# The second block's first projections on unscaled tiles, with their additive part from small products; two norms in one factor; the convolution begun on ScalarE

## The chip, the cores and the metric

The kernel runs on one core of a Trainium2 chip as one program. The metric is the device time of one execution in microseconds. Three runs of the kernel before took 2013.33, 2015.04 and 2018.52 us; the median is 2015.04.

## The reference

Two models follow each other on a sequence of 512 tokens of width 1024. The first has two layers, each with a root-mean-square norm, an input projection, three mixers, an output projection, a second norm and a gated feed-forward part of width 2816. After them stands a final norm. The second model is one block. What bears on the change is its start:

```python
x = rmsnorm(x, final_norm)                          # end of the first model
mod = silu(c) @ w_c + b_c                           # second model
shift, scl, gate = split(mod, 3)
h = rms_norm(x, g_pre) * (1 + scl) + shift
xa, za, q, k, v, zb, ga, gb = split(h @ w_in)
xa = centred_dwconv(xa, conv_w, conv_b)             # 4 taps along the tokens
... recurrences on xa, neighbourhood attention on q, k, v, gates, projections
x = x + gate * (merged @ w_o)
return rms_norm(x, g_final)
```

Both norms divide each token by the root of its mean square over the 1024 channels, with 1e-6 added under the root. `mod` depends on no token.

## The kernel before

**Layout.** Activations lie with channels on the 128 partitions and the 512 tokens along the free dimension, as 8 tiles of 128x512. Every projection is a sum over 8 or 11 such tiles. To keep float32 precision, each activation tile and each weight tile is held as a high and a low part in the replicated 32-bit format, and each product is three matmuls: high weights with the high tile (L404), high weights with the low tile (L407), low weights with the high tile (L408). `gemm` issues the 24 or 33 matmuls of one 128x512 output, and with `fresh` it waits for each tile's low part (`h_lo`).

**Weights.** `stream_plan` (L113) is the fixed order of 278 weight slots of 8 tiles of 128x128. SyncE loads them into a ring of four raw buffers. GpSimd splits each one into high and low parts (`split`, L2087): the high part by a multiplication with one, either with a tile of ones (L2097, two input tensors) or with a constant (L2099), and the low part by a subtraction (L2103). `parts_of` (L2109) chooses into how many pieces the 1024 columns are cut and which multiplication is used. GpSimd may split a slot when TensorE has begun the slot three places before it (`slot_used`), so it can be at most four ahead.

**The end of the first model.** In the last down projection VectorE adds each of the 8 outputs to x (L1858); ScalarE squares x, and x times the final gain (L1245), and VectorE sums both kinds of squares over the tiles (`add_twin_squares`). Two products with a matrix of ones (`stats`, L429, each in two passes) sum them over the partitions. Then comes a chain in which nothing else runs: ScalarE makes the first norm's factor with Ln and Exp, each with a table load (L949, L1248), VectorE multiplies twice (L1882, L1884), ScalarE makes the second factor (L1251, L1253), VectorE multiplies again (L1887), and then 8 tiles are made one after the other: xc by VectorE (L1891), the high part with the additive `shift` by ScalarE (L1258), the low part by VectorE (L1897). TensorE takes them as they come in the first output of `xa`. Then VectorE scales the 8 tiles of x by the first norm (L1902).

**The second block.** TensorE makes xa 0 to 7 in banks m % 4. For each, VectorE copies the bank into a padded row (L1912), makes the first tap (L1914) and adds the other three (L1918). Then a loop over t makes q, k, v, z and za of channel tile t, alternating between banks 0 and 1, with the attention of tile t-1 between them and four gate products (L893) at the end of each turn. q 0 is evacuated by VectorE (L1992), k 0 by ScalarE (L1305). VectorE executes its instructions in the written order, so q 0 is evacuated after the whole convolution. At the end stand 16 gates and 16 products `pa` and `pb`, and the output projection `wo` with a last norm (`inverse_rms`, L949, and L1372).

**The output projection of each layer** of the first model has 8 slots. After each output VectorE adds it to x (L1787), makes the low part of x times a gain (L1427) and adds the squares to a running sum (L1400). The feed-forward part starts on these unscaled tiles, and the factor is applied to its outputs.

Of the kernel before, what the change touches and what calls it, by code (L numbers as in the profile page):

```python
# [48 lines left out]
LAG = 2  # L49
MOD_SLOTS = 3 * KT  # L50
# [85 lines left out]
def build(nc, a_x, a_w, a_cmp, a_mod, a_c, a_const, a_misc, a_vec, a_rgw, a_rpb, a_out):  # L136
# [7 lines left out]
    with ctx:  # L144
# [39 lines left out]
        gainm = sb("gainm", [P, KT])  # L184
        arena = place[0]
# [32 lines left out]
        y_hi = sb("y_hi", [P, KT, S], F32R)  # L218
        y_lo = sb("y_lo", [P, KT, S], F32R)
# [19 lines left out]
        decay_sq = [asq[:, :], xpad[:, 0:S]]  # L239

# [106 lines left out]
        c_ready = Signal("c_ready")  # L347
        out_ok = Signal("out_ok")
# [32 lines left out]
        def _(pe):  # L381
# [41 lines left out]
            def stats(key, which=0):  # L423

                b = (7, 0)[which]
# [434 lines left out]
            for t in range(KT + 1):  # L860
                p = t - 1
                for place_, part in enumerate(("q", "k", "v", "z", "za")):
                    if t < KT:
                        gemm((part, t), gb % 2, a_hi, a_lo)
                        gb += 1
                    elif place_ < AHEAD:
                        gemm(("gate", place_), gb % 2, a_hi, a_lo)
                        gb += 1
# [15 lines left out]
                if t < KT:  # L884

                    pe.wait_ge(rgw_in, 16 * (t + 1))
                    if t == 0:

                        pe.wait_ge(to_pe.sem, to_pe.seen_by("pe"))
# [7 lines left out]
            for n in range(2 * KT):  # L897

                gemm(("prod", n), 2 + n % 2, y_hi, y_lo, fresh=0 if n % KT == 0 else None)
                if n + AHEAD < 2 * KT:  # L900
                    gemm(("gate", n + AHEAD), gb % 2, a_hi, a_lo)
                    gb += 1
            for m in range(KT):
                gemm(("wo", m), m % 4, a_hi, a_lo, fresh=0 if m == 0 else None)
# [38 lines left out]
        def _(act):  # L943
            A = nc.scalar.activation

            def inverse_rms(key, n, dst=None, src=None):
                act.wait_ge(*filling(key))
# [293 lines left out]

            for k in range(KT):
# [4 lines left out]
            inverse_rms(("n1",), D)  # L1247
            A(rstd[:, :], rstd[:, :], ACT.Exp, scale=-0.5).then_inc(rstd_ok.sem, 1)  # L1248
            act.wait_ge(rstd_ok.sem, rstd_ok.raised())
            act.wait_ge(to_act.sem, to_act.seen_by("act"))  # L1250
            A(tmp[:, :], tmp[:, :], ACT.Ln, scale=1.0 / D, bias=epst[:, 0:1]).then_inc(act_chain.sem, 1)  # L1251
# [4 lines left out]
            for k in range(KT):  # L1256
                act.wait_ge(to_act.sem, to_act.seen_by("act"))
                A(a_hi[:, k, :], xc[:, k, :], A_ID, bias=modv[:, k:k + 1]).then_inc(h_hi.sem, 1)  # L1258
                act.wait_ge(h_hi.sem, h_hi.raised())

# [103 lines left out]
            for m in range(KT):  # L1364
                act.wait_ge(to_act.sem, to_act.seen_by("act"))
                A(a_hi[:, m, :], merged[:, m, :], ACT.Copy).then_inc(h_hi.sem, 1)
# [10 lines left out]
        def _(dve):  # L1377
# [47 lines left out]
            def low_normed(k, gain):  # L1425
# [3 lines left out]
                dve.wait_ge(h_lo.sem, h_lo.raised())  # L1429

# [907 lines left out]
```

## Time and profile before

| | |
|---|---|
| median of three runs | 2015.04 us |
| the profiled execution's own time | 2021.89 us |
| its span | 2020.1 us |
| mean granted TensorE clock | 0.973 |
| TensorE busy | 1903.6 us (94%) |
| VectorE, ScalarE, GpSimd busy | 1154.3, 626.6, 1451.3 us |

The rows further down are of this one execution. Times are microseconds from the first instruction. PE is TensorE, DVE VectorE, ACT ScalarE, POOL GpSimd. A timeline row has start, duration, engine, line, operation, output and inputs, shape and count; instructions that follow each other are merged, and their duration is that of the group. In square brackets stands how long the engine was idle before, and what released it. TensorE's matmuls overlap, so the distance of two starts is the cost of one, not the duration shown.

### The profile page before, as it was taken

How to read it: one execution, taken by the hardware profiler on the slowest of the kernel's cores; microseconds unless marked ns; L12 is line 12 of the kernel's file. 1: busy time of each engine (PE TensorE's matmuls, PEld its weight loads, DVE VectorE, ACT ScalarE, POOL GpSimd, SP SyncE). 2: the span in 40 equal slices, each digit the busy share in tenths (PEclk: the TensorE clock that was granted, in tenths of full speed). 3: DMA queues.
4: the chain of work that ended last, by engine and by line, in shares of the span. 5: the costliest groups of instructions: out<-in, count | busy, mean ns of one | idle time of the engine just before them, and what ended most of it. 6: DMA issues, size and time to landing. Idle time of an engine off the chain costs nothing.

```text
span 2020.1 us, 27449 instructions
## 1 busy us (share of the span) xinstructions
PE 1903.6 (94%) x9982; PEld 1480.2 (73%) x9982; DVE 1154.3 (57%) x1656; ACT 626.6 (31%) x1134; POOL 1451.3 (72%) x998
## 2 busy tenths in 40 slices
PE   7999889999999999988999999996999999989996
PEld 5776557888888877755678888885777777778785
DVE  5756856576256357578465604654946666740343
ACT  4316652110011132267321101113036565540111
POOL 8963216798888897620478878885899888768893
PEclk9999889999999999999899999998999999999998
DMA  5241003343344222300124333532222332322321
GB/s 198 74 146 32 12 22 94 123 137 104 98 131 125 94 74 85 124 22 12 59 88 125 126 97 102 153 114 68 67 85 86 90 92 81 88 63 94 94 94 42
DMA packets 68687, 182.49 MB, mean 90 GB/s; under 512 B 23888, under 2 KB 24144, under 8 KB 68432
## 3 DMA queue, kind: packets, MB, share of 16 engines
q1 hardware_dynamic: 60480, 154.48, 24.9%
q10 hardware_dynamic: 8080, 26.32, 4.1%
q8 instruction: 80, 1.31, 0.3%
q14 instruction: 47, 0.39, 0.1%
HBM read 178.67 MB, written 2.10 MB: 89 GB/s over the span
## 4 chain that ended last, share of the span: by engine, by line
PE 68%; DVE 19%; ACT 8%; issue 4%; DMA 1%; ACTq 0%; DVEq 0%
PE PS L404 21%; PE PS L408 20%; PE PS L407 20%; DVE tmp L1400 2%; DVE a_lo L1427 2%; DVE xc L1918 1%; ACT P L1268 1%; DVE work L1680 1%; DVE PS L1631 1%; ACT rg L1339 1%; PE PS L646 1%; DVE rg L1975 1%; PE PS L531 1%; PE PS L684 1%; DVE rg L1978 1%
## 5 line engine op out<-in xcount | busy, mean ns | idle before, releaser
L2103 POOL TENSOR_TENSOR w_lo<-raw,w_hi 128x256 fp32r<-128x256 f32 (+2 forms) x582 | 777.6, 1336 | 46.5
L404 PE MATMUL PS<-a_hi,w_hi 128*128 128x512 f32 x1616 | 650.6, 403 | 42.5 <-POOL w_lo L2103 12.1
L2097 POOL TENSOR_TENSOR w_hi<-raw,const 128x1024 fp32r<-128x1024 f32 (+1 forms) x242 | 406.8, 1681 | 342.2 <-PE PS L404 329.8
L408 PE MATMUL PS<-a_hi,w_lo 128*128 128x512 f32 x1616 | 633.7, 392 | 0.0
L407 PE MATMUL PS<-a_lo,w_hi 128*128 128x512 f32 x1616 | 633.7, 392 | 0.0
L404 PEld LDWEIGHTS PS<-a_hi,w_hi 128*128 128x128 f32 x1616 | 305.6, 189 | 129.7 <-issue 37.9
L2099 POOL TENSOR_SCALAR w_hi<-raw 128x512 fp32r<-128x512 f32 x170 | 268.7, 1581 | 147.3 <-PE PS L404 139.8
L408 PEld LDWEIGHTS PS<-a_hi,w_lo 128*128 128x128 f32 x1616 | 305.8, 189 | 65.9
L407 PEld LDWEIGHTS PS<-a_lo,w_hi 128*128 128x128 f32 x1616 | 306.3, 190 | 64.1 <-issue 3.6
L1802 DVE TENSOR_TENSOR work<-PS,rstd 128x512 f32<-128x512 f32 x88 | 60.8, 691 | 146.7 <-PE PS L408 138.9
L404 PE MATMUL PS<-f_hi,w_hi 128*128 128x512 f32 x352 | 138.7, 394 | 0.0
L408 PE MATMUL PS<-f_hi,w_lo 128*128 128x512 f32 x352 | 138.0, 392 | 0.0
L407 PE MATMUL PS<-f_lo,w_hi 128*128 128x512 f32 x352 | 136.6, 388 | 0.0
L1233 ACT ACTIVATE work<-work 128x512 f32<-128x512 f32 x44 | 27.9, 633 | 313.6 <-DVE small L1806 313.5
L1858 DVE TENSOR_TENSOR x<-PS,x 128x512 f32<-128x512 f32 x32 | 22.1, 692 | 153.8 <-PE PS L408 153.7
L1813 DVE TENSOR_TENSOR f_lo<-work,f_hi 128x512 fp32r<-128x512 f32 x44 | 87.0, 1976 | 36.5 <-ACT f_hi L1236 36.5
L1236 ACT ACTIVATE f_hi<-work 128x512 fp32r<-128x512 f32 x44 | 27.8, 632 | 207.4 <-DVE work L1809 207.4
L1809 DVE TENSOR_TENSOR work<-work 128x512 f32<-128x512 f32 x44 | 86.4, 1964 | 2.3 <-ACT work L1233 0.9
L646 PE MATMUL PS<-const,work 128*128 128x128 f32 x320 | 59.6, 311 | 27.7 <-DVE work L1680 21.3
L646 PEld LDWEIGHTS PS<-const,work 128*128 128x128 f32 x320 | 38.1, 153 | 64.5 <-DVE work L1680 55.5
L408 PEld LDWEIGHTS PS<-f_hi,w_lo 128*128 128x128 f32 x352 | 66.1, 188 | 15.5
L407 PEld LDWEIGHTS PS<-f_lo,w_hi 128*128 128x128 f32 x352 | 66.1, 188 | 14.8
(295 smaller groups left out, 2535.9 us busy)
## 6 DMA issues: line engine op xcount, KB each, us to landing
raw<-weights SPq DMA_DIRECT2D x278, 512.0 KB, 3.5
work<-mod_w ACTq DMA_DIRECT2D x24, 512.0 KB, 3.6
work<-cmp_w ACTq DMA_DIRECT2D x8, 1024.0 KB, 5.8
bias<-rpb SPq DMA_DIRECT2D x256, 12.0 KB
rgw<-rgw ACTq DMA_DIRECT2D x8, 256.0 KB, 2.7
out<-xc SPq DMA_DIRECT2D x8, 256.0 KB, 2.1
const<-const SPq DMA_DIRECT2D x1, 1436.5 KB, 15.1
x<-x_t SPq DMA_DIRECT2D x4, 256.0 KB, 6.9
```

The costliest lines, as they stand in the source:

```text
L404: ins = nc.tensor.matmul(out, wh, hi, start=start, stop=False)
L407: nc.tensor.matmul(out, wh, lo, start=False, stop=False)
L408: return nc.tensor.matmul(out, wl, hi, start=False, stop=stop)
L646: ins = nc.tensor.transpose(PS[:, 4 + hh, n * P:(n + 1) * P], work[:, 2 * br + hh, n * P:(n + 1) * P], ident)
L1400: ins = TT(sums2[0], sq[:, 0, :] if k == 1 else sums2[0], sq[:, k % 2, :], ALU.add)
L1427: STT(a_lo[:, k, :], x[:, k, :], gain[:, k:k + 1], a_hi[:, k, :].bitcast(F32), ALU.mult, ALU.subtract).then_inc(h_lo.sem, 1)
L1802: TT(work[:, w0 + f % 2, :], PS[:, b0 + f % 2, :], rstd[:, :], ALU.mult)\
L1809: TT(work[:, 4 + f % 2, :], work[:, f % 2, :], work[:, 2 + f % 2, :], ALU.mult)\
L1813: TT(f_lo[:, f, :], work[:, 4 + f % 2, :], f_hi[:, f, :].bitcast(F32), ALU.subtract)\
L2097: G.tensor_tensor(w_hi[:, r, k, :], raw[:, r, k, :], ones[:, k, :], ALU.mult).then_inc(pool_chain, 1)
L2099: G.tensor_scalar(w_hi[:, r, k, :], raw[:, r, k, :], 1.0, None, ALU.mult).then_inc(pool_chain, 1)
L2103: ins = G.tensor_tensor(w_lo[:, r, k, :], raw[:, r, k, :], w_hi[:, r, k, :].bitcast(F32), ALU.subtract)
```

## The change

(1) `modulation`, the small operations on `modv`, moves ahead of the last down projection's evacuations and also splits `shift` into a high and a low part. ScalarE and VectorE make a_hi and a_lo there, tile by tile, from x times one combined gain.

(2) xa 0, 1 and 2 are computed from these unscaled tiles. Each of their 8 steps has two more matmuls, with two columns of `shift`, into bank 4. The two `stats` products stand before the last step of xa 0. The outputs are multiplied with the token factor on VectorE and get the additive part on ScalarE.

(3) The two norms' factors are one expression: with s1 and s2 the two sums, the factor is (s2/D + eps s1/D + eps^2) to the power -1/2. The shifted and scaled tiles are now b_hi and b_lo in other memory, and the y tiles take the place of a_hi and a_lo.

(4) ScalarE evacuates xa 3 to 7 and makes the first tap of all 8; VectorE makes the other three. There are two padded rows. The scaling of x by the first norm moves to after the evacuation of q 0.

(5) `load_ln` makes ScalarE load the Ln table by a one-column operation before it waits for the sums, in every norm.

(6) `parts_of`: the xa slots go from two pieces with a tile of ones to two high and four low pieces with the constant; the slots `out` 2 to 7 and the first two `gate` and `up` slots of a layer go from one piece to two with the constant; six slots around the first `pa` and the first `pb` use the constant in two pieces, and the slots from eight before `pa` 0 on have two pieces.

```diff
+EARLY = 3
@@ memory
-        y_hi = sb("y_hi", [P, KT, S], F32R)
-        y_lo = sb("y_lo", [P, KT, S], F32R)
+        b_hi = sb("b_hi", [P, KT, S], F32R)
+        b_lo = sb("b_lo", [P, KT, S], F32R)
+        y_hi, y_lo = a_hi, a_lo
...
+        padded = [xpad[:, :], rg[:, 0:2, :].rearrange("p a b -> p (a b)")[:, 0:S + 3]]
@@ TensorE
-            stats(("n1",), 0)
-            stats(("n2",), 1)
-            for m in range(KT):
-                gemm(("xa", m), m % 4, a_hi, a_lo, fresh=0 if m == 0 else None)
...
+            for m in range(EARLY):
...
+                for k in range(KT):
+                    if m == 0:
+                        if k == KT - 1:
+                            stats(("n1",), 0)
+                            stats(("n2",), 1)
+                        pe.wait_ge(h_lo.sem, h_lo.seen_by("pe"))
...
+                    nc.tensor.matmul(out, wh, a_lo[:, k, :], start=False, stop=False)
+                    nc.tensor.matmul(extra, wh, shift[:, k, 0:2], start=k == 0, stop=False)
+                    extra_ins = nc.tensor.matmul(extra, wl, shift[:, k, 2:4], start=False, stop=k == KT - 1)
...
+                    ins = nc.tensor.matmul(out, wl, a_hi[:, k, :], start=False, stop=k == KT - 1)
+            for m in range(EARLY, KT):
+                gemm(("xa", m), m % 4, b_hi, b_lo, fresh=0 if m == EARLY else None)
@@ ScalarE
+            def load_ln():
+                A(warm[:, :], epst[:, 0:1], ACT.Ln).then_inc(act_chain.sem, 1)
...
             def inverse_rms(key, n, dst=None, src=None):
+                load_ln()
...
+                A(a_hi[:, k, :], x[:, k, :], ACT.Copy, scale=gainm[:, k:k + 1]).then_inc(h_hi.sem, 1)
...
+            for m in range(KT):
+                row = padded[m % 2]
+                if m < EARLY:
+                    act.wait_ge(*emptying(("xa", m)))
+                    A(row[:, 2:S + 2], row[:, 2:S + 2], A_ID, bias=shifted[:, m:m + 1]).then_inc(act_chain.sem, 1)
...
+                else:
+                    act.wait_ge(conv_ok.sem, m - 1)
+                    act.wait_ge(*filling(("xa", m)))
+                    A(row[:, 2:S + 2], PS[:, m % 4, :], ACT.Copy).then_inc(emptied(("xa", m)), 1)
...
+                A(xc[:, m, :], row[:, 0:S], A_ID, scale=v_("conv_w")[:, m:m + 1], bias=v_("conv_b")[:, m:m + 1])\
+                    .then_inc(conv_begun.sem, 1)
...
+            inverse_rms(("n1",), D)
@@ VectorE
+            TS(tmp[:, :], PS[:, 7, :], EPS / D, EPS * EPS, ALU.mult, ALU.add).then_inc(dve_chain.sem, 1)
...
+            STT(tmp[:, :], PS[:, 6, :], 1.0 / D, tmp[:, :], ALU.mult, ALU.add).then_inc(emptied(("n2",)), 1)
...
+            dve.wait_ge(*filling(("shift",)))
+            V.tensor_reduce(shifted[:, :], PS[:, 4, 0:2 * EARLY].rearrange("p (m c) -> p m c", c=2), AX.X, ALU.add)\
+                .then_inc(emptied(("shift",)), 1)
...
+                TT(padded[m % 2][:, 2:S + 2], PS[:, m % 4, :], tmp[:, :], ALU.mult).then_inc(emptied(("xa", m)), 1)
@@ GpSimd
+            turns = [PLAN.index((kind, 0)) for kind in ("pa", "pb")]
...
-                if n == 0 or kind in ("pa", "pb", "wo") or kind == "in2" and not KT <= m < 6 * KT:
-                    return 2, 2
-                if kind in ("in", "in2") or kind == "out" and m < 2:
-                    return 2, 4
-                return 1, 1
+                if kind in ("in", "in2") and n < turns[0] - 2 * AHEAD and n or kind == "out" and m < 2:
+                    return 2, 4, True
+                if kind == "out" or kind in ("gate", "up") and m < 2 or any(-2 <= n - at < 4 for at in turns):
+                    return 2, 2, True
+                if n and kind in ("gate", "up", "down"):
+                    return 1, 1, False
+                return 2, 2, False
```

## Rows read from the trace of the kernel before

**Rows 1.** The page, busy time of each engine

```profile
PE 1903.6 (94%) x9982; PEld 1480.2 (73%) x9982; DVE 1154.3 (57%) x1656; ACT 626.6 (31%) x1134; POOL 1451.3 (72%) x998
```

**Rows 2.** Windows; columns us, busy us (x) per engine, PEclk, DMA share, GB/s

```profile
1391.00:1422.00 31.00, 13.82 (x25) 6.64 (x25) 20.95 (x27) 14.92 (x18) 6.02 (x4) 0.61 0.14 43
```

**Rows 3.** Timeline of TensorE, 1390 to 1497 us; start us, us

```profile
1390.40 0.40 PE L408 MATMUL PS<-f_hi,w_lo 128*128 128x512 f32 x1
...
1408.81 0.76 PE L404 MATMUL PS<-a_hi,w_hi 128*128 128x512 f32 x1 [11.30 <-issue]
...
1426.40 0.39 PE L404 MATMUL PS<-a_hi,w_hi 128*128 128x512 f32 x1
...
1431.84 0.39 PE L404 MATMUL PS<-a_hi,w_hi 128*128 128x512 f32 x1
...
1475.07 0.50 PE L404 MATMUL PS<-a_hi,w_hi 128*128 128x512 f32 x1 [2.95 <-DVE qkv L1992]
...
1493.16 3.59 PE L893 MATMUL PS<-xc,rgw 128*128 128x512 f32 x8
1496.19 0.80 PE L404 MATMUL PS<-a_hi,w_hi 128*128 128x512 f32 x1
```

**Rows 4.** Timeline of ScalarE, the table load for the second norm

```profile
1401.56 1.28 ACT L1251 ACT_TABLE_LOAD   x1 [1.58 <-DVE tmp L1884]
```

**Rows 5.** Timeline of VectorE, 1406 to 1448 us

```profile
1406.35 1.54 DVE L1891 SCALAR_TENSOR_TENSOR xc<-x,gainm,tmp 128x512 f32<-128x512 f32 x2
...
1420.50 1.64 DVE L1897 SCALAR_TENSOR_TENSOR a_lo<-xc,modv,a_hi 128x512 fp32r<-128x512 f32 x2
...
1435.73 4.55 DVE L1918 SCALAR_TENSOR_TENSOR xc<-xpad,vec,xc 128x512 f32<-128x512 f32 x3
...
1447.78 2.91 DVE L1918 SCALAR_TENSOR_TENSOR xc<-xpad,vec,xc 128x512 f32<-128x512 f32 x3
```

**Rows 6.** Groups by line and form, GpSimd; columns count, busy us, mean ns

```profile
L2103 POOL TENSOR_TENSOR w_lo<-raw,w_hi 128x1024 fp32r<-128x1024 f32 x144 | 364.5, 2531 | 11.3
L2097 POOL TENSOR_TENSOR w_hi<-raw,const 128x1024 fp32r<-128x1024 f32 x144 | 295.9, 2055 | 268.9 <-PE PS L404 266.1
L2103 POOL TENSOR_TENSOR w_lo<-raw,w_hi 128x256 fp32r<-128x256 f32 x340 | 273.6, 805 | 27.5
L2099 POOL TENSOR_SCALAR w_hi<-raw 128x512 fp32r<-128x512 f32 x170 | 268.7, 1581 | 147.3 <-PE PS L404 139.8
L2103 POOL TENSOR_TENSOR w_lo<-raw,w_hi 128x512 fp32r<-128x512 f32 x98 | 139.5, 1424 | 7.7
L2097 POOL TENSOR_TENSOR w_hi<-raw,const 128x512 fp32r<-128x512 f32 x98 | 110.8, 1131 | 73.3 <-PE PS L404 63.8 <-DMA const<-const 5.7
```

**Rows 7.** Timeline of GpSimd around the second block's start

```profile
1374.69 1.04 POOL L2097 TENSOR_TENSOR w_hi<-raw,const 128x512 fp32r<-128x512 f32 x1 [0.47 <-PE PS L404]
...
1447.44 1.66 POOL L2099 TENSOR_SCALAR w_hi<-raw 128x512 fp32r<-128x512 f32 x1
...
1454.81 1.93 POOL L2099 TENSOR_SCALAR w_hi<-raw 128x512 fp32r<-128x512 f32 x1
```

**Rows 8.** Timeline of TensorE, 155 us, eight 64-column products

```profile
155.03 1.10 PE L656 MATMUL PS<-kblk,proj 128*128 128x64 f32 x8
```

**Rows 9.** Timeline of TensorE, turn from layer 0 to layer 1

```profile
711.58 1.02 PE L429 MATMUL PS<-tmp,const 128*128 128x512 f32 x2
```

**Rows 10.** Timelines of VectorE and TensorE, end of layer 1's output projection

```profile
1027.18 2.74 DVE L1400 TENSOR_TENSOR tmp<-tmp,sq 128x512 f32<-128x512 f32 x1
1029.96 0.69 DVE L1787 TENSOR_TENSOR x<-PS,x 128x512 f32<-128x512 f32 x1
...
1031.49 0.50 PE L404 MATMUL PS<-a_hi,w_hi 128*128 128x512 f32 x1 [3.07 <-DVE a_lo L1427]
```

**Rows 11.** Timelines of TensorE and ScalarE, the last norm

```profile
2006.15 1.10 PE L429 MATMUL PS<-tmp,const 128*128 128x512 f32 x2 [2.51 <-DVE tmp L1400]
...
2007.35 1.28 ACT L949 ACT_TABLE_LOAD   x1 [2.14 <-PE PS L429]
```

More of the change, by code:

```diff
@@ L423, in stats @@
             def stats(key, which=0):
-                b = (7, 0)[which]
+                b = (7, 6)[which]
                 if claim(key, b):
@@ L863, in _ @@
                     if t < KT:
-                        gemm((part, t), gb % 2, a_hi, a_lo)
+                        gemm((part, t), gb % 2, b_hi, b_lo)
                         gb += 1
                     elif place_ < AHEAD:
-                        gemm(("gate", place_), gb % 2, a_hi, a_lo)
+                        gemm(("gate", place_), gb % 2, b_hi, b_lo)
                         gb += 1
@@ L900, in _ @@
                 if n + AHEAD < 2 * KT:
-                    gemm(("gate", n + AHEAD), gb % 2, a_hi, a_lo)
+                    gemm(("gate", n + AHEAD), gb % 2, b_hi, b_lo)
                     gb += 1
             for m in range(KT):
-                gemm(("wo", m), m % 4, a_hi, a_lo, fresh=0 if m == 0 else None)
+                gemm(("wo", m), m % 4, b_hi, b_lo, fresh=0 if m == 0 else None)
             stats(("n3",))
@@ L1854, in _ @@
                     gain = v_("g_attn")[:, (l + 1) % DEPTH * KT:]
+                    if last and l + 1 == DEPTH:
+                        modulation()
                     for m in range(KT):
@@ L1896, in _ @@
                     dve.wait_ge(h_hi.sem, h_hi.seen_by("dve"))
-                    STT(a_lo[:, j, :], xc[:, j, :], modv[:, j:j + 1], a_hi[:, j, :].bitcast(F32),
+                    STT(b_lo[:, j, :], xc[:, j, :], modv[:, j:j + 1], b_hi[:, j, :].bitcast(F32),
                         ALU.add, ALU.subtract).then_inc(h_lo.sem, 1)
                     dve.wait_ge(h_lo.sem, h_lo.raised())
-            for k in range(KT):
-                STT(x[:, k, :], x[:, k, :], v_("g_fin1")[:, k:k + 1], rstd[:, :], ALU.mult, ALU.mult)\
-                    .then_inc(dve_chain.sem, 1)
-                dve.wait_ge(dve_chain.sem, dve_chain.raised())
@@ L1994, in _ @@
                     dve.wait_ge(*emptying(("q", t)))
+                if t == 0:
+                    dve.wait_ge(rstd_ok.sem, rstd_ok.seen_by("dve"))
+                    for k in range(KT):
+                        STT(x[:, k, :], x[:, k, :], v_("g_fin1")[:, k:k + 1], rstd[:, :], ALU.mult, ALU.mult)\
+                            .then_inc(dve_chain.sem, 1)
+                        dve.wait_ge(dve_chain.sem, dve_chain.raised())
                 if p >= 0:
```

118 lines of the change are left out of this document (80 added, 38 removed).

## The prediction

> **What bounds the kernel now.** I read the page's engine totals first. TensorE is busy 94% of 2020.1 us [rows 1], so only a stretch in which it stands still, or runs at its lower clock, can give much back. The windows show one such stretch, 1391 to 1422 us: TensorE works 13.8 of 31 us at a mean granted clock of 0.61, which is a mix of 1.2 and 2.4 GHz after a long idle time [rows 2]. TensorE's timeline says what it is. The last product of layer 1's down projection starts at 1390.40, so the next could start at 1390.63; the first product of xa 0, the second block's first projection, starts at 1408.81. It starts again after a stop at 1475.07, where v 0 waits until VectorE, late from the convolution, has emptied bank 0. The gate products of channel tile 0 run from 1493.16, and q 1 begins at 1496.19 [rows 3]. I take 1390.63 to 1496.19, 105.6 us, as the stretch that the change rebuilds. At full speed one weight slot (24 products) takes 5.44 us: 1426.40 and 1431.84 are the same place in two successive slots [rows 3].
>
> **The stretch rebuilt, TensorE's own work.** Thirteen slots (xa 0 to 7, q, k, v, z, za of tile 0) are 13 x 5.44 = 70.7 us. Two sums over partitions stay: one took 1.02 us inside a running stream [rows 9], so 2.0. The gate products stay at 3.0 (1493.16 to 1496.19). New are 3 x 8 x 2 = 48 two-column products, each with its own 128x128 weight load. The trace has no two-column product. The nearest row is eight 64-column products with such loads in 1.10 us, 0.14 each [rows 8]; two columns cannot use the load's time better, so I take 0.13, 6.2 us in all. Bounds: 0 if the loads hide, 48 x 5.44/24 = 10.9 if each costs as much as a full product. Sum 81.9 us, against 105.6 before: 23.7 us, if nothing waits.
>
> **Does something wait? The start.** xa 0 needs no factor any more, only x times a gain, which ScalarE and VectorE make tile by tile while the down projection still runs. The turn from layer 0 to layer 1 has this form already, and there the sums' products start at 711.58 in the middle of a running stream [rows 9]. Only the last tile is late, and seven of eight k steps of xa 0 stand before it (7 x 0.94 = 6.6 us). The seven small operations on modv move in front of the down evacuations, a microsecond or so under 7.5 us of products. I count no wait.
>
> **The second norm.** Its two norms are now one expression, so one Ln and one Exp remain. The sums end at 1390.6 + 6.6 + 2.0 = 1399.2. From the load for Ln to the first xc tile the old second half took 1401.56 to 1406.35 [rows 4, 5]; less the load (1.28, now made ahead) and one product (0.7), plus one new VectorE operation (0.7), that is 3.5: 1402.7. Then 8 xc and 8 b_lo tiles. Before they took 1406.35 to 1422.14, 15.8 us; the three convolution steps, the same kind of operation, took 2.91 beside constant-multiply splits, 0.97 each, and 4.55 beside two-tensor splits, 1.52 each [rows 5]. With 0.97 and a gap of 0.04, 16 are 16.2 us: b_lo 7 at 1419. TensorE wants it for the last k of xa 3 at 1390.6 + 3 x 7.5 (a slot with its 16 small products) + 2.0 + 4.8 = 1420, and bank 0 for xa 4 at 1420.6, which VectorE empties 0.8 us after b_lo 7. So this chain is hidden by less than a microsecond. I count 0.7 us. Here the small products are cover too: were they free, xa 4 would still wait for VectorE, so their lower bound is worth about 5 us less than it looks.
>
> **The convolution.** ScalarE now evacuates and makes the first tap, and VectorE keeps three steps (2.9 us) and, for three tiles, one evacuation, under 5.44 us a slot. Started at 1420, it ends about 5 us after xa 7's last product. q 0 is emptied before v 0 wants the bank, and the 2.95 us stop goes with the low clock behind it. The eight scalings of x move behind q 0 on VectorE, which stood idle there; the norm's factor for them on ScalarE comes before k 0's evacuation. Cost nothing; if VectorE is 5 us later than I think, the old stop returns, 3 to 5 us.
>
> **The supply of weights** comes next. GpSimd splits each slot. By mean durations [rows 6] the old form of an xa slot costs 2 x (1.13 + 1.42) = 5.1 us, the new one 2 x 1.58 + 4 x 0.81 = 6.4, and beside a busy VectorE 1447.44 to 1454.81 = 7.4 [rows 7]; TensorE uses a slot in 5.44. GpSimd starts xa 0 at 1374.69 and is never ahead again. The thirteenth slot, za 0, is then ready at 1374.7 + 13 x 6.4 = 1457.9 or, at 7.4, at 1470.9; TensorE wants it at 1390.6 + 22.6 + 2.0 + 9 x 5.44 = 1464.2. Bounds 0 and 6.7 us. VectorE has pauses after 1425, so I take 3 us. In this stretch 23.7 - 0.7 - 3 = 20 us are left.
>
> **The other edits.** (a) The last norm: its Ln table load, 1.28 us from 2007.35 with nothing beside it [rows 11], goes ahead of the sums' result, for which ScalarE has waited 2.14 us. Gain 1.3. The same edit at the other norms is beside running products: nothing. (b) Output projection, both layers: VectorE's running sum takes 2.74 us there, stuck behind 1024-wide two-tensor splits, and the last residual add starts only at 1029.96, directly behind it; TensorE waits 3.07 us for a_lo [rows 10]. TensorE stands from 1028.4 (1031.49 - 3.07), so the add could start near 1028.6. With 512-wide splits half of them constant multiplies VectorE is free in time. That gives 1.3 us a layer, bounds -1 (four short operations each held once) and 3.1; I take 1.2 twice, 2.4. Its price: ten slots a layer go from 4.6 to 6.0 us or, beside VectorE's two operations a slot, about 6.3. GpSimd falls back 10 x 0.86 = 8.6 us and has 3 x 5.44 - 6.3 = 10 in hand: nothing, just. (c) The forms at the turns to pa and pb: TensorE hardly waits there; nothing. (d) The y tiles' change of place moves no instruction.
>
> Sum 20 + 1.3 + 2.4 = 23.7 us. The profiled execution took 2021.89, so it would take 1998; it lies 6.85 above the median of the runs, 2015.04, and on that the forecast is 1991.3.
>
> **A rule weighed.** The rows say that a constant multiply on GpSimd does not hold VectorE back: a three-step group began at 1447.78, 0.34 us after a 1.66 us constant multiply, and was over at 1450.69 [rows 5, 7]. Had its first step waited for 1449.10, three steps of 0.77 (two took 1.54) would have ended after 1451.4. The Trainium skill (SBUF — State Buffer, Who interferes with whom) says that a VectorE instruction with two SBUF inputs contends with any GpSimd instruction that reads SBUF, and the loser blocks for the whole of it. By that rule the new form would free nothing, and rival 1 would be the case; the trace disagrees with it for this form.
>
> **Rivals.** 1. *VectorE's chain is what xa 3 waits for.* Its steps then cost 1.52, not 0.97 [rows 5]: 16 x 1.56 = 25 us, b_lo 7 at 1427.7, 7.7 us late; with (b) giving nothing 23.7 - 7 - 2.4 leaves 14.3, 2001. For it: all sixteen read two tensors, and GpSimd, busy for only 6 of 31 us there before [rows 2], now works throughout. Against it: the 2.91 row. 2. *Supply binds.* Slots at 7.4 throughout here lose 3.7 us more, and at 6.8 in (b) they lose 10 x 1.36 - 9.5 = 4 a layer: 12 left, 2003. For it: GpSimd without any idle time. Against it: VectorE's pauses. 3. *Slower: the output projection starves.* If ten slots a layer cost 8 us there, TensorE loses 10 x 2.56 - 8.3 = 17 a layer, 34; 13 slots of 8 end at 1478.7, 14.5 us late: 25 - 34 - 14.5 is a loss of 23.5, 2038.5. With only the 3 us here it turns at about 7.4 us a slot there. For it: constant multiplies are the slowest form per element. Against it: 6.3 expected, and 7.4 seen only for the form with six operations beside a VectorE without pauses. 4. *The edit does less than it says*: a wait at xa 0 that I don't see (GpSimd's or the last tile's) leaves half, 2004. 5. *Better*: small products at half price and supply free, 1984 to 1986.
>
> **Numbers.** Forecast (1986 to 1998) 0.56, better 0.10, rivals 1 and 2 0.10 each, rival 4 0.04, cases that end within 6 us of 2015 0.05, rival 3 0.05. The range 1984 to 2005 leaves out the ends. 0.3%, 6 us, is what a measurement can tell: faster 0.90, same 0.05, slower 0.05.
>
> **What would show it.** Right: no TensorE gap over 1 us from 1380 to 1420; 48 products at 0.13; q 1 near 1476; no wait at v 0; the running sum in the output projection under 1.6 us; the last table load before the sums. Wrong: small products above 0.2; GpSimd named as releaser anywhere after the start; xa 3 or xa 4 waiting for VectorE by over 2 us; or a TensorE wait in the output projection above 3 us.

## The result and the profile after

The changed kernel takes 1985.43 us (median of four runs, 1984.21 to 1988.35) against 2016.3 us for the kernel before beside it (2013.33 to 2018.52): a ratio of 0.985, 95% interval 0.9832 to 0.9868, a gain of 30.9 us. The forecast was 1991.3, a gain of 23.7. The profiled execution took 1985.22 us, with a span of 1983.3. Its engine totals, to set against [rows 1] (busy us, share of the span, instructions), show TensorE busy for 13.6 us less though it makes 48 products more, and GpSimd busy for 51 us more:

```profile
PE 1890.0 (95%) x10030; PEld 1478.4 (75%) x10030; DVE 1118.3 (56%) x1657; ACT 645.5 (33%) x1165; POOL 1502.5 (76%) x1046
```

The idle stretch of [rows 2] is gone. The windows of the kernel after, first the 31 us that begin at the same place of the work, then 5 us in k 0 (busy us and count of each engine, granted clock, DMA share, GB/s):

```profile
1377.00:1408.00 31.00, 30.83 (x154) 24.86 (x154) 25.62 (x32) 13.20 (x18) 29.28 (x26) 1.00 0.28 88
1437.00:1442.00 5.00, 5.00 (x16) 3.98 (x15) 4.83 (x5) 0.00 (x0) 4.75 (x4) 0.66 0.31 108
```

TensorE works 30.83 of 31 us at full clock, where it worked 13.82 at 0.61. GpSimd, idle there before, works 29.28 of the 31 us, and that matters below.

I cut both traces at the same instructions of TensorE and compared the stages. Each length is a difference of two starts, in us; the stages not shown differ by less than 1 us each:

| stage | before | after | gain | forecast |
|---|---|---|---|---|
| end of the down projection to q 1 (the rebuilt stretch) | 105.56 | 89.16 | 16.4 | 20 |
| output projections, both layers | 58.58 + 58.34 | 53.96 + 53.96 | 9.0 | 2.4 |
| feed-forward parts | 363.52 + 356.18 | 360.04 + 354.59 | 5.1 | 0 |
| pa 0 to wo 0 (pa, pb and the gates between) | 158.99 | 154.15 | 4.8 | 0 |
| end, from the last norm's sums on | 13.94 | 12.64 | 1.3 | 1.3 |
| whole span | 2020.1 | 1983.3 | 36.8 | 23.7 |

The profiled execution of before lay 5.6 us above its median, so 36.8 here answers to 30.9 in the timed runs. The forecast total was 7 us short, because four errors partly cancelled: one term too big by 3.6 us, one too small by 6.6 us, and two counted as nothing.

Half of the 5.1 us of the feed-forward parts belongs to the row above it. In the kernel before, the low clock that follows TensorE's wait at the end of the output projection reaches into the feed-forward part. Here are the same 5 us of layer 0 in the kernel before and in e3, which has only the output projection's new forms (us, TensorE busy and products, clock, DMA share, GB/s):

```profile
348.00:353.00 5.00, 5.00 (x12) 0.53 0.00 0
```

```profile
348.00:353.00 5.00, 5.00 (x23) 1.00 0.42 142
```

The two parts take 361.34 and 355.81 us in e3, so 2.2 and 0.4 us go with that wait; the other 1.3 and 1.2 us are the memory layout (e1 and e2).

**The start of the second block.** TensorE's timeline of the kernel after (start, duration, engine, line, operation, output and inputs, shape, count, idle time before and its releaser):

```profile
1376.38 0.39 PE L419 MATMUL PS<-f_hi,w_lo 128*128 128x512 f32 x1
1376.60 0.39 PE L808 MATMUL PS<-a_hi,w_hi 128*128 128x512 f32 x1
...
1377.06 0.17 PE L812 MATMUL PS<-shift,w_hi 128*128 128x2 f32 x1
1377.08 0.25 PE L813 MATMUL PS<-shift,w_lo 128*128 128x2 f32 x1
...
1383.00 1.02 PE L440 MATMUL PS<-tmp,const 128*128 128x512 f32 x2
1383.86 1.02 PE L440 MATMUL PS<-work,const 128*128 128x512 f32 x2
...
1436.47 0.47 PE L415 MATMUL PS<-b_hi,w_hi 128*128 128x512 f32 x1 [1.88 <-POOL w_lo L2188]
...
1437.49 0.63 PE L418 MATMUL PS<-b_lo,w_hi 128*128 128x512 f32 x1
...
1440.88 0.39 PE L415 MATMUL PS<-b_hi,w_hi 128*128 128x512 f32 x1
...
1457.21 0.47 PE L415 MATMUL PS<-b_hi,w_hi 128*128 128x512 f32 x1 [0.60 <-POOL w_lo L2188]
...
1465.77 0.80 PE L415 MATMUL PS<-b_hi,w_hi 128*128 128x512 f32 x1
```

xa 0 begins 0.22 us after the last down product starts; in [rows 3] it began 18.4 us after. Seven k steps with two small products each take 6.40 us (1376.60 to 1383.00), 0.914 each; one without takes 0.68, so a two-column product with its own weight load costs 0.117 us in place of the 0.13 forecast. q 1 begins at 1465.77. At the start of k 0 TensorE waits 1.88 us for GpSimd, and from 1437.49 to 1440.88 its products are 0.42 us apart: the granted clock stood at 0.66 over those 5 us, a mix of the two levels 1.2 and 2.4 GHz, after that wait and a smaller one (0.45 us, at q 0) had broken the stream. v 0, z 0 and za 0 (1457.21) begin with a wait for GpSimd too, 0.81, 0.60 and 0.60 us.

**Who TensorE waits for in that stretch** (the waits view, 1372 to 1470: total us, times, longest):

```profile
PE PS L415 <- POOL w_lo L2188: 4.3, 5, 1.9
PE PS L415 <- DVE b_lo L1975: 0.2, 1, 0.2
```

**GpSimd there.** The first row begins the split of xa 0, the last ends that of za 0, the thirteenth slot. Between the two in the middle lies one slot (two multiplications, four subtractions):

```profile
1360.84 1.49 POOL L2182 TENSOR_SCALAR w_hi<-raw 128x512 fp32r<-128x512 f32 x1 [0.43 <-PE PS L415]
...
1416.53 1.81 POOL L2182 TENSOR_SCALAR w_hi<-raw 128x512 fp32r<-128x512 f32 x1
...
1424.71 1.81 POOL L2182 TENSOR_SCALAR w_hi<-raw 128x512 fp32r<-128x512 f32 x1
...
1455.54 1.53 POOL L2188 TENSOR_TENSOR w_lo<-raw,w_hi 128x256 fp32r<-128x256 f32 x2
```

A slot takes 7.5 to 8.2 us while VectorE works through the convolution. TensorE uses one in 5.44. The 13 slots take GpSimd 96.2 us (1360.84 to 1457.07), 7.40 each, without a pause. From q 0 on it sets the pace: each of the last five slots begins on TensorE 0.14 us after its split has ended.

### The profile page after: what moved, and what is told of

It is laid out like the page before. It is cut to its first block, busy times and chain, and to the rows that moved or that the text cites. A ratio compares the mean times of both kernels' runs of the same rounds, so it can differ in the third digit from the quotient of the medians.

```text
span 1983.3 us, 27653 instructions
## 1 busy us (share of the span) xinstructions
PE 1890.0 (95%) x10030; PEld 1478.4 (75%) x10030; DVE 1118.3 (56%) x1657; ACT 645.5 (33%) x1165; POOL 1502.5 (76%) x1046
## 4 chain that ended last, share of the span: by engine, by line
PE 70%; DVE 12%; ACT 8%; POOL 5%; issue 4%; DMA 1%; ACTq 0%; DVEq 0%; POOLq 0%
PE PS L415 21%; PE PS L419 21%; PE PS L418 21%; POOL w_lo L2188 2%; POOL w_hi L2182 2%; ACT P L1326 1%; DVE work L1755 1%; DVE PS L1706 1%; ACT rg L1397 1%; PE PS L657 1%; PE PS L695 1%; PE PS L542 1%; DVE rg L2057 1%; DVE tmp L1458 1%; DVE rg L2054 1%
## 5 line engine op out<-in xcount | busy, mean ns | idle before, releaser
L2182 POOL TENSOR_SCALAR w_hi<-raw 128x512 fp32r<-128x512 f32 x242 | 390.6, 1614 | 292.6 <-PE PS L415 282.0
L415 PE MATMUL PS<-a_hi,w_hi 128*128 128x512 f32 x1168 | 463.6, 397 | 17.8 <-POOL w_lo L2188 12.0
L419 PE MATMUL PS<-a_hi,w_lo 128*128 128x512 f32 x1168 | 456.2, 391 | 0.0
L418 PE MATMUL PS<-a_lo,w_hi 128*128 128x512 f32 x1168 | 456.1, 391 | 0.0
L415 PE MATMUL PS<-b_hi,w_hi 128*128 128x512 f32 x552 | 223.1, 404 | 5.9 <-POOL w_lo L2188 4.3
L418 PE MATMUL PS<-b_lo,w_hi 128*128 128x512 f32 x552 | 216.0, 391 | 0.0
L419 PE MATMUL PS<-b_hi,w_lo 128*128 128x512 f32 x552 | 215.6, 391 | 0.0
L415 PEld LDWEIGHTS PS<-b_hi,w_hi 128*128 128x128 f32 x552 | 104.0, 188 | 38.1 <-issue 13.2
L419 PEld LDWEIGHTS PS<-b_hi,w_lo 128*128 128x128 f32 x552 | 104.1, 189 | 22.3
L418 PEld LDWEIGHTS PS<-b_lo,w_hi 128*128 128x128 f32 x552 | 104.0, 188 | 21.9 <-issue 1.9
```

The lines of the kernel that those rows point to most:

```text
L415: ins = nc.tensor.matmul(out, wh, hi, start=start, stop=False)
L418: nc.tensor.matmul(out, wh, lo, start=False, stop=False)
L419: return nc.tensor.matmul(out, wl, hi, start=False, stop=stop)
L2182: G.tensor_scalar(w_hi[:, r, k, :], raw[:, r, k, :], 1.0, None, ALU.mult).then_inc(pool_chain, 1)
```

## The experiments

Each was timed in five rounds beside the kernel before. They ran in three groups, each on one chip: the changed kernel again, e1, e2 and e3 (the kernel before had a median of 2020.46 us there); e4, e5, e6 and e8 (2018.3); e7, e9, e10 and e11 (2020.66). Medians are compared within a group, and between groups only by their ratios to the kernel before, whose intervals are 3 to 4 us wide on each side. The length of the stretch comes from the profile of each run and repeats well: 89.14 to 89.24 us in the five profiles that keep the changed kernel's form of it, 104.4 in e1 and e3, which keep that of the kernel before (105.56 in its own).

**The changed kernel again**, as the base of the first group.

> The changed kernel again, as the yardstick for the others on this chip: 30 to 32 us faster than before.

1985.64 us, 0.9825 (0.981 to 0.984), stretch 89.16 us, as in the first profile.

**e1, the place in memory alone.** The changed kernel has 192 bytes more per partition ahead of its large tiles (`shift`, `shifted`, `warm`). Here the kernel before gets an unused tile of that size.

```diff
+        pad = sb("pad", [P, 48])
```

> The kernel before with an unused tile of 192 bytes in front of the tiles that start with proj, f_hi and y_hi, so that these lie where the changed kernel has them; no instruction differs. Theory A (place in memory): in both profiles products that read a_hi are 226.7 ns apart in the feed-forward part, but those that read f_hi, proj_r or y_hi are 229.0 to 229.4 apart before and 226.7 after. Then this kernel alone has 226.7 everywhere and is 4 to 5 us faster than before. Rival B (the spacing follows from the splits on GpSimd or from what runs beside): still 229, 0 us.

2016.03 us, 0.9975 (0.9962 to 0.9988): 4.4 us faster by an unused tile. **e2** is the reverse, 64 bytes more in the changed kernel.

```diff
+        pad = sb("pad", [P, 16])
```

> The changed kernel with an unused tile of 64 bytes in front of the same tiles, which puts them back to the alignment of before. Theory A: products from f_hi, proj_r and b_hi 229 ns apart, 4 to 5 us slower than the changed kernel. Rival B: no difference.

1994.01 us, 0.9868 (0.9851 to 0.9885), 8.4 us slower than the changed kernel beside it. Fifty microseconds inside a down projection, first the kernel before, then e1, then e2 (window, TensorE busy and number of products, clock, DMA share, GB/s):

```profile
470.00:520.00 50.00, 50.00 (x220) 1.00 0.30 95
```

```profile
470.00:520.00 50.00, 50.00 (x222) 1.00 0.32 102
```

```profile
470.00:520.00 50.00, 50.00 (x220) 1.00 0.30 98
```

TensorE is 100% busy at full clock in all three, and yet makes 220 products or 222. From single starts the spacing is 229.0 to 229.4 ns in the one case and 226.7 in the other. The moving tiles with the larger spacing (f_hi, proj_r, y_hi before; f and b tiles in e2) lie 64 bytes behind a multiple of 128, those with the smaller one on a multiple of 128. (This is worked out from the sizes of the tiles, counted from the first one, x.) So a part of the gain is the memory layout and not the edits. In the profiles that differ in layout but not in the low clock before them, it is 1.3 us in the first feed-forward part and 1.2 in the second (e2 and e3 take 361.3 and 355.8, the changed kernel and its variants 360.0 and 354.6 every time), and in the stage of pa and pb 1.8 (e1) and 1.4 (e2). e1's own profile is 2.7 us better than before in the first feed-forward part, but half of this is a shorter stretch at the low clock (0.91 and not 0.53 from 348 to 353) and not the layout. The two runs put the layout's whole at 4 and 8 us in the medians, and with intervals of 3 us and more on each side the two are not different.

**e3, the output projection's forms alone**, in the kernel before.

```diff
+                if kind == "out" or kind in ("gate", "up") and m < 2:
+                    return 2, 2, True
```

> The kernel before with one part of the change: the slots out 2 to 7 and the first two gate and up slots of each layer are split in two pieces with the constant multiply. Theory C: VectorE was one whole slot (5.5 us) behind at the end of the output projection, and the wait of TensorE for a_lo (3.5 us to the next start, plus the lower clock behind it) goes in both layers: 8 to 11 us faster than before, residual add of out 7 directly behind its last product. The prediction's reading was 2.4 us. Rival: GpSimd falls behind and TensorE waits for it, under 2 us gained.

2010.62 us, 0.9949 (0.9933 to 0.9964): 9.8 us faster, where I had counted 2.4. In its profile the two output projections take 8.6 us less and the feed-forward parts behind them 2.6. Its VectorE and TensorE timelines at the end of layer 1's output projection, as for [rows 10]:

```profile
1020.97 0.69 DVE L1787 TENSOR_TENSOR x<-PS,x 128x512 f32<-128x512 f32 x1 [3.00 <-PE PS L408]
...
1023.10 0.98 DVE L1400 TENSOR_TENSOR tmp<-tmp,sq 128x512 f32<-128x512 f32 x1
...
1026.71 1.10 PE L429 MATMUL PS<-tmp,const 128*128 128x512 f32 x2 [0.39 <-DVE tmp L1400]
```

The last residual add now waits for its product, and not the other way round. The sum's products come with a gap of 0.39 us in place of the 3.07.

**e4, the forms of xa and the rule.** xa 0 to 7 get pieces of 512 columns and the multiplication with a tile of ones.

```diff
             def parts_of(n):
                 kind, m = PLAN[n][0], PLAN[n][-1]
+                if kind == "in2" and m < KT:
+                    return 2, 2, False
```

> The changed kernel with the eight xa slots split as before (two pieces, multiplied with a tile of ones). Theory D: in the changed kernel GpSimd took up to 8.2 us for a slot beside VectorE and TensorE waited for it five times from v 0 on (4.3 us, and about 2 us at the lower clock). In the old form a slot costs about 6, so these waits go; but VectorE's steps rise from about 1.0 to 1.5 us, b_lo 7 comes some 7 us later and TensorE waits for it in xa 3 and xa 4. Net within 2 us of the changed kernel. Rival E (VectorE's chain has room): 5 us faster. Rival F (the old form is worse on both): 5 us or more slower.

The first of the five waits that this names stands at q 0, and v 0 has the third. 1986.31 us, 0.9835 (0.9815 to 0.9854), against 0.9825 of the changed kernel: no difference that can be told. The stretch is 89.80 us, 0.6 longer. The view of the line that makes xc, in e4 and then in the kernel after (minimum, median, maximum of a step in ns, first and last start):

```profile
L1969 DVE SCALAR_TENSOR_TENSOR xc<-x,gainm,tmp x8: 751/1657/1662, 1392.0 to 1409.2; 128x512 f32<-128x512 f32 x8
```

```profile
L1969 DVE SCALAR_TENSOR_TENSOR xc<-x,gainm,tmp x8: 750/930/1169, 1388.8 to 1402.3; 128x512 f32<-128x512 f32 x8
```

And TensorE's waits in the stretch, in e4:

```profile
PE PS L415 <- DVE b_lo L1975: 3.7, 2, 2.2
PE PS L415 <- POOL w_lo L2188: 0.9, 2, 0.6
```

The two-tensor form frees GpSimd and holds VectorE. It trades one wait for the other at about the same price. e4 changes the multiplication and the width of the subtractions at once; e5, next, has the wide subtractions with the constant, and the same step has a median of 0.98 us there and a longest of 1.66. So it is the two-tensor multiplication that holds every step, and a wide subtraction holds those that meet it.

**e5: 512 columns and the constant multiply** for xa 0 to 7 (as e4, with `return 2, 2, True`).

> The changed kernel with the eight xa slots in two high and two low pieces, constant multiply. One slot has two operations fewer: 0.4 us less alone, perhaps 0.8 beside VectorE. Theory D: GpSimd reaches z 0 three to six microseconds earlier, TensorE's waits from v 0 on shrink, 3 to 5 us faster than the changed kernel; VectorE's steps stay near 1.0. Rival: a 512-wide subtraction holds VectorE longer each time, b_lo 7 late, no gain.

1980.38 us, 0.9813 (0.9793 to 0.9834): 5.9 us faster than e4 in its group. The stretch is 85.67 us, 3.5 shorter than in the changed kernel. TensorE's waits there:

```profile
PE PS L415 <- POOL w_lo L2188: 1.9, 2, 1.3
PE PS L415 <- DVE b_lo L1975: 1.5, 1, 1.5
```

**e9 and e10** go on with this form: to the first 13 slots (e9: xa, and q, k, v, z, za of channel tile 0), and to all slots of that loop (e10: `kind == "in2" and m < 6 * KT`).

```diff
+                if kind == "in2" and (m < KT or m % KT == 0 and m < 6 * KT):
+                    return 2, 2, True
```

> The changed kernel with the thirteen slots of this stretch (xa 0 to 7 and q, k, v, z, za of tile 0) in two high and two low pieces, constant multiply. With the xa slots alone in this form the stretch went from 89.2 to 85.7 us, and 1.9 us of waits for GpSimd stayed at the tile-0 slots, which beside the convolution still took up to 8.2 us each. Theory D (supply is what is left): 2 us less again, stretch near 83.5, some 7 us faster than the changed kernel; the floor is TensorE's own 81.5. Rival: VectorE, held longer by each 512-wide subtraction, ends the convolution late and v 0 waits for q 0's bank again, no gain over the form for xa alone.

> As the last one, but with every slot of the loop over t in that form too. Theory: a turn of the loop is TensorE's own work (38.5 us) and GpSimd has slack in it, so the loop's 303 us stay within 1 us. Rival: the fewer, longer subtractions hold VectorE in the loop, 2 us or more slower there.

e9: 1978.29 us, 0.9794 (0.9775 to 0.9813), stretch 83.27. e10: 1977.87 us, 0.9794 (0.9776 to 0.9813), stretch 83.24, and the rest of the loop as it was (303.8 us in place of 303.4): the later slots need nothing. Both beat the kernel before by 42 us, and e7 and e11 of their group, which keep the changed kernel's forms, by 7 to 9. The stretch accounts for 5.9 of it; their profiles are also 2.7 us shorter in layer 1's mixers, which the edit does not touch. They are the best of all that ran. TensorE's waits and GpSimd's slots of e9:

```profile
PE PS L415 <- DVE b_lo L1975: 1.5, 1, 1.5
```

```profile
1415.10 1.81 POOL L2182 TENSOR_SCALAR w_hi<-raw 128x512 fp32r<-128x512 f32 x1
...
1422.10 1.81 POOL L2182 TENSOR_SCALAR w_hi<-raw 128x512 fp32r<-128x512 f32 x1
```

A slot is 7.0 us in place of 8.2, and over the 13 slots 6.83 in place of 7.40. No wait for GpSimd is left, and the stretch lies 2.0 us above TensorE's own work of 81.3 us (worked out below).

**e6, less work for TensorE.** The small products of xa 0 to 2 run in the last k step only, so this kernel leaves out most of the additive part.

```diff
-                    nc.tensor.matmul(extra, wh, shift[:, k, 0:2], start=k == 0, stop=False)
-                    extra_ins = nc.tensor.matmul(extra, wl, shift[:, k, 2:4], start=False, stop=k == KT - 1)
+                    if k == KT - 1:
+                        nc.tensor.matmul(extra, wh, shift[:, k, 0:2], start=True, stop=False)
+                        extra_ins = nc.tensor.matmul(extra, wl, shift[:, k, 2:4], start=False, stop=True)
```

> The changed kernel with 6 of the 48 two-column products; the additive part of xa 0 to 2 is left out but for the last channel tile. They were 0.12 us each by the starts in the trace, 5 us in all. Theory D (supply binds in this stretch): TensorE comes earlier to the same wait for GpSimd, and under 1.5 us is gained. Rival (TensorE's own work binds): 5 us faster than the changed kernel.

1984.49 us, 0.9835 (0.9816 to 0.9855). 42 of 48 small products are gone, 5 us of TensorE's time, and the stretch is 0.2 us shorter (88.95). TensorE only met its waits earlier:

```profile
PE PS L415 <- POOL w_lo L2189: 4.1, 5, 1.9
PE PS L415 <- DVE b_lo L1976: 2.5, 3, 1.3
```

The wait for VectorE took 2.3 us more, and a second stretch at the low clock, from 1401.6 to 1405.0, about 1.6. The end is still GpSimd's: its split of za 0 is done 80.2 us after the down projection, where it was 80.5, and TensorE begins za 0 0.14 us later.

**e11, more work for VectorE.** The convolution's first tap goes back to VectorE.

```diff
-                A(xc[:, m, :], row[:, 0:S], A_ID, scale=v_("conv_w")[:, m:m + 1], bias=v_("conv_b")[:, m:m + 1])\
+                A(warm[:, :], epst[:, 0:1], ACT.Copy)\
...
+                TS(xc[:, m, :], padded[m % 2][:, 0:S], cw[:, m:m + 1], v_("conv_b")[:, m:m + 1], ALU.mult, ALU.add)\
+                    .then_inc(dve_chain.sem, 1)
+                dve.wait_ge(dve_chain.sem, dve_chain.raised())
```

> The changed kernel with the convolution's first tap on VectorE again (ScalarE still evacuates). Eight more VectorE operations of 0.7 to 1.5 us. Theory: the convolution then ends 6 to 10 us later, q 0 is emptied late, v 0 waits for it, and of this only what exceeds the supply's own delay shows: 3 to 6 us slower than the changed kernel. Rival (supply hides it): under 1 us.

1987.14 us, 0.9833 (0.9816 to 0.985), stretch 88.99. q 0's evacuation, the first thing behind the convolution, began 4.6 us later than in the kernel after, each counted from the end of its down projection (1376.60 and 1377.63). The kernel after first, then e11:

```profile
1434.70 1.08 DVE L2071 TENSOR_SCALAR qkv<-PS 128x512 f32<-128x512 f32 x1 [1.34 <-PE PS L419]
```

```profile
1440.36 1.14 DVE L2074 TENSOR_SCALAR qkv<-PS 128x512 f32<-128x512 f32 x1
```

The rival was right, my own expectation wrong: while the supply is late, this delay lies beside the wait for weights and costs nothing in the stretch.

GpSimd's slots beside the convolution take 7.3 to 8.1 us here, 7.5 to 8.2 in the changed kernel, and took 7.4 to 7.6 in the kernel before [rows 7]. In that order VectorE had, for each channel tile, one operation with a single tensor input (the first tap), none, and two (the copy and the first tap) between its two-input steps. So a slot may be dearer the fewer of these light operations are left. That is a reading of three kernels and not a test, and in sum it did not slow the supply: with the first tap on VectorE the convolution lasts longer, more slots lie beside it, and the 13 take 7.39 us each against 7.40. In the changed kernel ScalarE's first tap buys nothing by itself; whether it would with e9's forms was not tried.

**e7, the last norm's table load** not made ahead.

```diff
-                load_ln()
+                if key != ("n3",):
+                    load_ln()
```

> The changed kernel with the last norm's Ln table loaded after the sums again. The prediction's term: 1.3 us slower than the changed kernel, all of it behind the last sums' product (12.6 us to the end becomes 13.9). The Trainium skill (ScalarE: Activation LUTs, What ACT_TABLE_LOAD costs) gives 2.66 us for a switch, so by that page 2.7 us slower.

1985.33 us, 0.9823 (0.9806 to 0.9841). The medians cannot tell 1.3 us, but the trace can. ScalarE at the end of the kernel after, then in e7:

```profile
1969.85 1.28 ACT L981 ACT_TABLE_LOAD   x1
...
1971.90 0.69 ACT L988 ACTIVATE rstd<-PS,epst 128x512 f32<-128x512 f32 x1 [0.55 <-PE PS L440]
```

```profile
1974.38 1.28 ACT L989 ACT_TABLE_LOAD   x1 [2.14 <-PE PS L440]
1975.67 0.69 ACT L989 ACTIVATE rstd<-PS,epst 128x512 f32<-128x512 f32 x1
```

The sums' products start at 1970.70 and 1973.18. The factor follows 1.20 us later in the one and 2.49 in the other: 1.29 us, the load and little else, and not the 2.7 us that the expectation set beside it.

**e8, the forms at the turns to pa and pb** as before.

```diff
-                if kind == "out" or kind in ("gate", "up") and m < 2 or any(-2 <= n - at < 4 for at in turns):
+                if kind == "out" or kind in ("gate", "up") and m < 2:
```

> The changed kernel with the twelve slots around the first pa and the first pb split with the tile of ones as before. Theory G: these forms are why TensorE no longer waits for the low parts of y at the turn to pb (8.6 us for a 5.4 us slot before, 5.85 after): 2 to 3 us slower than the changed kernel, in that slot. The prediction had counted nothing for it. Rival: the waits went for another reason (place in memory), 0 us.

1991.24 us, 0.9867 (0.9845 to 0.9889, from four runs between 1988.85 and 1994.55): 5 and 7 us slower than e4 and e6 in its group, which keep the new forms there. The stage of pa and pb takes 157.21 us, not 154.15. Of the waits at the turn to pb, the first is the kernel before, the second e8; the kernel after has none there.

```profile
PE PS L404 <- DVE y_lo L2047: 1.9, 3, 0.7
```

```profile
PE PS L415 <- DVE a_lo L2132: 2.1, 4, 0.7
```

## Why the prediction was right, and where it was wrong

**The number, and how much of it was luck.** 1985.43 lies in the stated range, but below the band of the forecast itself (1986 to 1998), where I had put a "better" case: small products at half price and supply free. That is not what happened. The small products cost 0.117 us and the supply cost all that its upper bound allowed; the number came out low because the output projection, the turns and the memory layout gave what I had not counted. So the direction and most of the mechanism were foreseen, and that the total was only 7 us off is in part luck. Of my own signs, TensorE has no gap over 1 us at the start, the small products, the running sum and the last load came as written. q 1 begins 89.2 us after the down projection and not 85.4, v 0 still begins with a wait (0.81 us), and a sign of being wrong came true: GpSimd is named as releaser five times.

**The mechanism, and TensorE's own work: right.** The gap goes because xa 0 no longer waits for the norm. The first product and both sums run inside the stream, q 0 no longer waits for the convolution, and VectorE's stop at v 0 [rows 3] is gone; what stands there now is the supply's. The sum of own work was 81.9; with 0.117 us a small product it is 81.3 (70.7 + 2.0 + 3.0 + 5.6). The nearest row, 0.14 for 64 columns [rows 8], was a good guide.

**VectorE's chain behind the norm: right, with a smaller wait.** In the kernel after:

```profile
1388.83 1.96 DVE L1969 SCALAR_TENSOR_TENSOR xc<-x,gainm,tmp 128x512 f32<-128x512 f32 x2 [2.64 <-ACT tmp L1293]
...
1403.10 2.26 DVE L1975 SCALAR_TENSOR_TENSOR b_lo<-xc,modv,b_hi 128x512 fp32r<-128x512 f32 x2
```

The group's second step ends at 1405.36 with b_lo 7, 28.8 us after the down projection's end (1376.60); the forecast was 28.4 (1419 less 1390.6). TensorE waited 0.2 us, where I had 0.7. Rival 1, with steps of 1.52 us, falls: the steps here are 0.75 to 1.17. e4 is what it looks like when it is true: steps of 1.66 and 3.7 us of waits.

**The supply of weights: right mechanism, mis-sized.** This is the failed term of the stretch. I took 3 us, bounds 0 and 6.7, from slots of 6.4 to 7.4 us. It measured 89.16 less 81.3 less 0.2, about 7.7 us. What failed is the choice within the bounds and not the sum. GpSimd starts xa 0 15.8 us before the down projection's end, as in the kernel before (15.9), and is never ahead again; the 13 slots take 7.40 us each on average, single ones 6.3 to 8.2, where I had 7.4 as the dearest. za 0's split is ready at 1457.07, which is 1471.1 in the times of the kernel before, where the upper bound's sum has 1470.9. With 6.7 in place of 3 the stretch would have come to 16.3 us of gain; it is 16.4. I took 3 because VectorE has pauses after 1425 in the kernel before. In the kernel after the convolution ran without pauses to 1433.4, which is 1447 there, and GpSimd's slots were dear up to v 0.

In TensorE's rows only 4.3 of the 7.7 us are waits, and 1.6 are eight products at the low clock behind the longest (3.39 us in place of 8 x 0.227); the rest are small delays at each restart. But the low clock cost nothing of its own here: v 0 begins 0.14 us after its split is done, so without it TensorE would only have waited longer. Four experiments bear the cause out. Cheaper slots gain in the stretch, 3.5 us (e5, 7.13 us a slot) and 5.9 us (e9, 6.83), and less work on TensorE (e6) or more on VectorE (e11) changes it by 0.2 us each. In this stretch, rival 2 was the truer description; its other half, a loss of 4 us a layer in the output projection, did not occur.

**The output projection: wrong by a factor of four.** I read from [rows 10] that TensorE stands from 1028.4 and concluded that the last output was finished then, so that the residual add was at most 1.3 us late. But TensorE had gone on past it: in the kernel before

```profile
1023.94 0.39 PE L408 MATMUL PS<-proj_r,w_lo 128*128 128x512 f32 x1
1024.16 0.39 PE L404 MATMUL PS<-a_hi,w_hi 128*128 128x512 f32 x1
...
1028.03 0.39 PE L408 MATMUL PS<-a_hi,w_lo 128*128 128x512 f32 x1
```

The last product of the projection starts at 1023.94; the rows from 1024.16 to 1028.03 are six k steps of the next stage, on tiles that were ready; then comes the 3.07 us wait [rows 10]. After the change the add follows the start of that product by 0.50 us, so the add at 1029.96 was 5.5 us late, a whole slot, and these 4.1 us of useful work covered most of it. After the change:

```profile
1016.24 0.69 DVE L1862 TENSOR_TENSOR x<-PS,x 128x512 f32<-128x512 f32 x1 [2.95 <-PE PS L419]
...
1018.41 0.98 DVE L1458 TENSOR_TENSOR tmp<-tmp,sq 128x512 f32<-128x512 f32 x1
...
1022.02 1.10 PE L440 MATMUL PS<-tmp,const 128*128 128x512 f32 x2 [0.45 <-DVE tmp L1458]
```

The two stages are 9.0 us shorter and e3 alone gives 9.8 in the medians, 8.6 in these stages of its profile. VectorE's running sum went from 2.74 to 0.98 us. The 4.6 and 4.4 us of the two layers are more than my upper bound of 3.1, the visible wait. In layer 1 the waits fell from 3.3 us (a second one of 0.26 followed) to 0.5. Then comes the low clock behind them, which I had left out: in the kernel before

```profile
1031.83 0.49 PE L407 MATMUL PS<-a_lo,w_hi 128*128 128x512 f32 x1
...
1034.45 1.49 PE L429 MATMUL PS<-tmp,const 128*128 128x512 f32 x2
1035.37 0.80 PE L404 MATMUL PS<-a_hi,w_hi 128*128 128x512 f32 x1
```

From the restart at 1031.49 [rows 10] to 1034.45 there are six products; at full clock they and the 0.26 us of wait would take 1.6 us in place of 2.96. The sum's two passes took 0.92 us to the next start, in the kernel after 0.54. These are 1.7 us, with the 2.8 of waits 4.5. In layer 0 the low clock lasted longer, from 345.9 to 352.7, and took 2.2 us more in the feed-forward part. TensorE waits for GpSimd nowhere in that stage, so rival 3, the starved projection, did not occur.

**The last norm: right**, 1.3 forecast, 1.3 in the stage and 1.29 in e7.

**Counted at nothing, but not nothing.** (c) The forms at the turns were read as free because the waits there sum to 1.9 us. e8 shows 3.1 us in the stage; its median is 5 to 7 us worse, and what the rest is stays open. (d) The y tiles' change of place, I wrote, moves no instruction. That is true, but the three new small tiles in front move every large tile by 192 bytes, and TensorE's spacing with it: 4 us (e1) to 8 us (e2) in the medians. This was no part of the diff's stated content, and no view of the profile before would have priced it, though the 229 ns against 226.7 could be read in it. The terms don't add up as if they were separate: 16.4 + 9.8 + 1.3 + 3.1 + 4 to 8 are 35 to 39 us against 31 to 35 in the medians. The layout's share lies partly inside the stages of the others, and the profiled execution of before, from which the 16.4 comes, was a long one: against e1 and e3 (104.4) the stretch gains 15.2.

**The rule on the shared ports.** In the kernel after, GpSimd and VectorE:

```profile
1400.80 1.81 POOL L2182 TENSOR_SCALAR w_hi<-raw 128x512 fp32r<-128x512 f32 x1
```

```profile
1401.29 0.98 DVE L1975 SCALAR_TENSOR_TENSOR b_lo<-xc,modv,b_hi 128x512 fp32r<-128x512 f32 x1
```

The two-input step begins and ends while the constant multiply runs. Thirteen steps of the stretch do so, each in 0.98 us. Steps that begin in a 256-column subtraction take about 1.1 us, and beside the two-tensor operations of e4 the median is 1.66. The Trainium skill (SBUF — State Buffer, Who interferes with whom) has a VectorE instruction with two SBUF inputs contend with a GpSimd instruction that reads SBUF, for an exclusive lock; for the constant multiply these rows decide against it, as the prediction had it. The other direction cost more than I had thought: beside the convolution the same constant-multiply slot is 7.0 us or up to 8.2 by its piece size, against 6.4 from mean durations.

## What to carry to other kernels

A visible wait is not the lateness of what it waits for. Before pricing a late producer, find the last instruction of its true input and see what the consumer ran in between; here a wait of 3.1 us hid a lateness of 5.5. When an edit removes a long stall, price the engine that rested during it (here GpSimd) beside neighbours that never pause: after the stall it has no slack, and the dear end of its range is the one to take. To find what sets a stretch's length, compare the time at which each slot is ready with the time at which it is begun. If they stay a constant apart (0.14 us here), the producer sets the end, and what the consumer loses meanwhile, at a low clock too, costs nothing; where the consumer's own stream sets it, as in the output projection, add the low clock that follows each break. And if the edit adds even a small tile, compare the spacing of equal matmuls in the two traces before giving the gain to the edit.

## What the runs showed of the hardware

- A 512-column product is 226.7 ns from the next one, or 229.0 to 229.4 (1% more), by where its moving tile lies: on a multiple of 128 bytes from the first tile, or 64 behind one. Seen in e1, e2, before and after. Tried with these two offsets only.
- A two-column product with its own 128x128 weight load costs 0.117 us in a running stream (kernel after).
- GpSimd's constant multiply does not hold VectorE's two-input steps (0.98 us for 13 steps wholly inside one, a median of 1.66 beside two-tensor operations in e4), but is itself slowed: mostly 1.81 to 1.93 us where 1.49 is its undisturbed time for 128x512.
- Cutting the 1024 columns into two subtractions and not four makes a GpSimd slot 7.0 us in place of up to 8.2 beside a busy VectorE (e9).
- Making the table load ahead of the wait gave back 1.29 us for a load shown as 1.28 (e7).
